# Mix weights of a decoder step: the second half of w_out stays on the chip, the rest passes through one buffer, and TensorE spreads the sample's rows

## What is computed

```python
xn = rms_norm(x, g_mix)
z = xn @ w_in                       # q, k, v of A and B, gates ga, gb
oa, ob, state = mix_fn(qa, ka, va, qb, kb, vb, sink)
ya = oa.reshape(n, s, WIDTH_A) @ w_a          # 512 x 1024
yb = ob.reshape(n, s, WIDTH_B) @ w_b          # 512 x 1024
merged = jax.nn.sigmoid(ga) * ya + jax.nn.sigmoid(gb) * yb
h = x + merged @ w_o                          # 1024 x 1024
hn = rms_norm(h, g_ffn)
y = h + peer(hn.reshape(n * s, D_MODEL), w_pq, sub_keys, u_tab, v_tab).reshape(n, s, D_MODEL)
...
u = jnp.take(u_tab, eb, axis=0)               # peer: per token 128 rows of 1024
act = jax.nn.gelu(jnp.einsum('cd,ced->ce', xb, u, preferred_element_type=jnp.float32), approximate=False)
v = jnp.take(v_tab, eb, axis=0)
out = jnp.einsum('ce,ced->cd', (gb * act).astype(v.dtype), v, preferred_element_type=jnp.float32)
```

## Time and profile before

| | us |
|---|---|
| median of three runs (lowest, highest) | 2066.01 (2065.30, 2066.04) |
| the profiled execution | 2062.75 |
| its span in the trace | 2061.0 |
| TensorE busy | 1453.5 (71%) |
| VectorE busy | 1210.7 (59%) |
| GpSimd busy (issuing the gathers) | 1153.9 (56%) |
| ScalarE busy | 370.2 (18%) |
| traffic of the 16 DMA engines | 710.66 MB, mean 345 GB/s |
| granted clock of TensorE, mean | 0.842 of 2.4 GHz |

### The profile page before, as it was taken

The page is one execution under the profiler, slowest core; times in us unless marked ns, Lnnn a source line. Parts: engine busy times, 40 slices in busy tenths (PEclk is TensorE's granted clock), DMA queues, the critical chain, the costliest instruction groups (busy, mean ns, idle before and its releaser), DMA issues.

```text
span 2061.0 us, 18791 instructions
## 1 busy us (share of the span) xinstructions
PE 1453.5 (71%) x5438; PEld 653.7 (32%) x5438; DVE 1210.7 (59%) x3332; ACT 370.2 (18%) x905; POOL 1153.9 (56%) x1082
## 2 busy tenths in 40 slices
PE   8999898956947495858975566656556767644557
PEld 5443343543423252323332222222222323211111
DVE  1033351497666477656657667677667777776440
ACT  2113342322222121111111111111111111100000
POOL 2020000146656566665777777777677676767764
PEclk9999999967968697789998787888779888777779
DMA  9999987688998889999999999999999999999997
GB/s 335 362 326 370 355 276 245 222 283 316 400 396 326 311 328 379 360 365 370 367 378 383 345 356 356 350 372 364 330 355 363 339 352 348 363 374 382 353 357 276
DMA packets 227303, 710.66 MB, mean 345 GB/s; under 512 B 21288, under 2 KB 46792, under 8 KB 227176
## 3 DMA queue, kind: packets, MB, share of 16 engines
q0 software_dynamic: 166912, 612.40, 79.8%
q1 hardware_dynamic: 60288, 97.05, 13.6%
HBM read 704.84 MB, written 72.65 MB: 377 GB/s over the span
## 4 chain that ended last, share of the span: by engine, by line
PE 30%; issue 26%; DMA 14%; POOL 13%; DVE 10%; another core or an unknown queue 3%; ACT 2%; POOLq 1%; SPq 0%; DVEq 0%; ACTq 0%
PE bank L991 8%; POOL WR L618 7%; POOL XS L618 5%; DMA arena<-in_peer_u_dram,e_all 4%; PE bank L880 4%; DMA XS<-in_peer_u_dram,e_all 4%; DMA WR<-in_peer_v_dram,arena 4%; PE bank L1008 4%; DVE XS L1377 3%; PE bank L1086 3%; PE bank L1107 2%; POOL arena L618 2%; PE bank L1128 2%; PE bank L910 1%
## 5 line engine op out<-in xcount | busy, mean ns | idle before, releaser
L991 PE MATMUL bank<-WR,arena 128*64 128x512 f32 x2048 | 662.1, 753 | 372.6 <-DMA WR<-in_peer_v_dram,arena 245.6
L618 POOL DMA_INDIRECT WR<-in_peer_v_dram,arena x512 | 572.8, 1119 | 249.0 <-issue 161.2
L1377 DVE SCALAR_TENSOR_TENSOR XS<-XS,GT 128x1024 f32<-128x1024 f32 x384 | 465.4, 1225 | 290.8 <-DMA XS<-in_peer_u_dram,e_all 268.3
L618 POOL DMA_INDIRECT XS<-in_peer_u_dram,e_all x384 | 412.2, 1073 | 316.1 <-issue 123.3
L991 PEld LDWEIGHTS bank<-WR,arena 128*64 128x64 f32 x2048 | 184.6, 168 | 790.5 <-issue 752.1
L1377 DVE SCALAR_TENSOR_TENSOR arena<-arena,GT 128x1024 f32<-128x1024 f32 x128 | 157.0, 1226 | 23.4 <-DMA arena<-in_peer_u_dram,e_all 19.5
L618 POOL DMA_INDIRECT arena<-in_peer_u_dram,e_all x128 | 123.2, 963 | 42.2 <-issue 37.1
L1008 PE MATMUL bank<-WR,XS 128*128 128x512 f32 x256 | 118.1, 616 | 12.1 <-ACT GT L746 11.6
L880 PE MATMUL bank<-WR,XS 128*128 128x512 f32 x256 | 112.0, 595 | 0.0
L693 ACT ACTIVATE XS<-bank 128x256 f32<-128x256 f32 (+1 forms) x90 | 36.1, 403 | 361.2 <-remote 190.1
L932 PE MATMUL bank<-arena,PP 128*128 128x64 f32 x272 | 41.8, 282 | 69.2 <-issue 43.7
(11 more groups left out here) (208 smaller groups left out, 1694.7 us busy)
## 6 DMA issues: line engine op xcount, KB each, us to landing
out_dram<-in_cache_a_k_dram POOLq DMA_DIRECT2D x8, 4064.0 KB, 53.0
out_dram<-in_cache_a_v_dram POOLq DMA_DIRECT2D x8, 4064.0 KB, 52.4
WR<-in_w_in_dram SPq DMA_DIRECT2D x8, 2048.0 KB, 24.3
GT<-in_w_peer_q_dram SPq DMA_DIRECT2D x14, 1024.0 KB, 7.2
WR<-in_w_out_dram SPq DMA_DIRECT2D x6, 2048.0 KB
WR<-in_peer_v_dram,arena POOLq DMA_INDIRECT x512
WR<-in_w_branch_a_dram SPq DMA_DIRECT2D x6, 1024.0 KB
WR<-in_w_branch_b_dram SPq DMA_DIRECT2D x6, 1024.0 KB
```

The source lines that it names most:

```text
L618: nc.gpsimd.indirect_dma_start(dst, None, table, bass.IndirectOffsetOnAxis(ap=idx, axis=0))\
L991: last = nc.tensor.matmul(b[c][R * j:R * j + R, :], diag[v % 4][:, s % 4, :], V[V_AT[s]][:, c * CHUNK:(c + 1) * CHUNK], start=False, stop= ...
L1377: V_.scalar_tensor_tensor(u, u, 1.0, hidden[q // TILE_Q], ALU.mult, ALU.mult, accum_out=dots[:, s // TOPK % 4, s % TOPK:s % TOPK + 1]).the ...
```

## The change

1. **w_out's second half** is loaded into w_mix[1] in batch 0 and stays. The two loads of it for batches 1 and 2 are gone.
2. **The branch weights** of batches 1 and 2, both halves, go through w_mix[0]: half 1 is loaded once branches(t, 0) of the batch's last tile is done, then half 0 of w_out once branches(t, 1) is done. In SyncE's queue half 1 of batch 1 moves from behind half 0 to behind query_weights(5), and half 1 of batch 2 from behind half 0 to behind norm_final (L565), ahead of x_again(2).
3. **The mix pieces move** to other slots, and out(t, 1) comes before out(t, 0). post(3), the turn of tile 3's attention, moves from slot 70 to 69. The counts of the semaphore merged follow.
4. **The sample's rows** are spread by TensorE: in slots 143 to 149, sample_rows(b) is for each half one matmul of 512 columns with the identity's column b, broadcast to 128 columns, as the stationary side (8 partitions deep), and one copy by ScalarE of the bank into hbc. The copy's semaphore hb takes the place of the loads' hb_in. hn_scratch, its write and the eight broadcasts are gone.

Slots of the pieces, before and after (br0 is branches(t, 0) and so on):

| tile | before: br0, br1, merged, out0, out1 | after: br0, br1, merged, out1, out0 |
|---|---|---|
| 0 | 17, 18, 19, 19, 20 | 17, 18, 19, 19, 20 (out0 first, as before) |
| 1 | 38, 39, 41, 42, 43 | 38, 40, 42, 43, 44 |
| 2 | 55, 56, 58, 74, 75 | 67, 72, 73, 74, 75 |
| SAMPLE | 70, 71, 73, 76, 77 | 68, 72, 74, 75, 76 |
| 3 | 72, 73, 75, 78, 79 | 70, 73, 74, 75, 77 |

```diff
-    for t, (a, b, c, d, e) in {0: (17, 18, 19, 19, 20), 1: (38, 39, 41, 42, 43), 2: (55, 56, 58, 74, 75),
-                               SAMPLE: (70, 71, 73, 76, 77), 3: (72, 73, 75, 78, 79)}.items():
+    for t, (a, b, c, e, d) in {0: (17, 18, 19, 20, 19), 1: (38, 40, 42, 43, 44), 2: (67, 72, 73, 74, 75),
+                               SAMPLE: (68, 72, 74, 75, 76), 3: (70, 73, 74, 75, 77)}.items():
...
+    for b in range(DEC):
+        put(head_at(SAMPLE, PH - 1) + 1 + min(b, 6), "sample_rows", b)
...
             def branch_weights(batch, c):
+                b = c if batch == 0 else 0
                 if batch == 0:
                     filled(sp, "gate", GATES - 1 - (1 - c) * ALL, 0)
+                elif c == 0:
+                    filled(sp, "out", BATCHES[batch - 1][-1], 0, 0)
                 else:
-                    filled(sp, "out", BATCHES[batch - 1][-1], c, 0)
+                    filled(sp, "branches", BATCHES[batch][-1], 0, 1)
...
             def out_weights(batch, c):
-                filled(sp, "branches", BATCHES[batch][-1], c, 1)
+                filled(sp, "branches", BATCHES[batch][-1], c if batch == 0 else 1, 1)
...
             branch_weights(1, 0)
-            branch_weights(1, 1)
...
             for n in range(3, 6):
                 query_weights(n)
+            branch_weights(1, 1)
             out_weights(1, 0)
-            out_weights(1, 1)
             x_again(1)
             query_weights(6)
             query_weights(7)
             branch_weights(2, 0)
-            branch_weights(2, 1)
...
             query_weights(PH + 2)
-            x_again(2)
...
             sp.dma_start(gfin, g_fin.partition_broadcast(P)).then_inc(S["gfin_in"], 16)
+            branch_weights(2, 1)
+            x_again(2)
             x_again(SAMPLE)
             out_weights(2, 0)
-            out_weights(2, 1)
...
-            for b in range(DEC):
-                sp.dma_start(hbc[b], hn_scratch[b, :].partition_broadcast(P)).then_inc(hb_in[b], 16)
...
+                    elif stage == "sample_rows":
...
+                        for c in range(2):
+                            b = filled(act, "sample_rows", at[0], c)
+                            nc.scalar.activation(hbc[at[0]][:, c * CHUNK:(c + 1) * CHUNK], b[:, :], ACT.Copy).then_inc(S["hb"], 1)
...
+                        for c in range(2):
+                            b, landed = take("sample_rows", r, c)
+                            nc.tensor.matmul(b[:, :], ident[0:DEC, r:r + 1].to_broadcast([DEC, P]),
+                                             hidden[SAMPLE][0:DEC, c * CHUNK:(c + 1) * CHUNK], start=True, stop=True).then_inc(landed, 1)
```

More of the change, by code:

```diff
@@ L144 @@
 USES = {"gate": 1, "gate_sum": 1, "turned": 4, "post": 2, "sample_soft": 2, "sample_turn": 1, "sample_back": 1, "branches": 2, "merged": 2, "out": 1,
-        "hidden": 2, "query": 1, "score": 1, "sample_turn_lists": 2}
+        "hidden": 2, "query": 1, "score": 1, "sample_turn_lists": 2, "sample_rows": 2}
 def tensor_order(pieces, beside):
@@ L196 @@
 BATCH = {t: i for i, ts in enumerate(BATCHES) for t in ts}
-MIX_ORDER = {t: i for i, t in enumerate((0, 1, 2, SAMPLE, 3))}
+MERGED = {0: 2, 1: 4, 2: 8, SAMPLE: 9, 3: 10}
 def ring(slots, buffers):
@@ L360, in hybrid_step_kernel @@
         v_landed = [sem(f"v_landed{j}") for j in range(VR)]
-        hb_in = [sem(f"hb_in{b}") for b in range(DEC)]
         block = ctx.enter_context(nc.Block())
@@ L582, in _ @@
             answer(1)
-            sp.wait_ge(S["hn"], ALL)
-            sp.dma_start(hn_scratch, hidden[SAMPLE][0:DEC, :]).then_inc(S["hn_out"], 16)
             answer(2)
-            sp.wait_ge(S["hn_out"], 16)
-            filled(sp, "query", SAMPLE, PH - 1, 0)
-            for b in range(DEC):
-                sp.dma_start(hbc[b], hn_scratch[b, :].partition_broadcast(P)).then_inc(hb_in[b], 16)
             answer(3)
```

29 lines of the change are left out of this document (18 added, 11 removed).

## The result

| | before | after |
|---|---|---|
| median (lowest, highest), four runs each | 2065.66 (2054.88, 2066.04) | 2093.22 (2085.74, 2099.64) |
| the profiled execution, its span | 2062.75, 2061.0 | 2085.74, 2083.9 |

The ratio of after to before is 1.0145 (95% interval 1.0116 to 1.0175): slower by 1.5%, 20 us above the forecast of 2073, 13 us above 2080, the upper end of the forecast's own range, and 8 us above 2085, the end of the whole range. The direction was right, the size was not: +27.6 us instead of +7.

The account below looks back on a forecast made before the run. Gathers bound the kernel, paced by DMA at 11.96 us a slot, with TensorE the other limit from 931 to 1050 us. Terms 0 − 3 − 2 + 18.5 − 7 = +6.5, about +7 on the 2066.01 median: 2073, range 2056 to 2085.

Parts of the forecast that it names:

- part 2: Batch 2's loads, 561 to 608 us: 2.1 MB fewer, −3; two branches pieces leave slots 55 and 56, −2.
- part 1: Batch 1's loads, near 357 and 500 us: 0; query weights 8 us later, their wait priced in the next term.
- Part 3: Slot 68 on VectorE: SAMPLE's gating waits for gb_in, gathers resume near 928 instead of 917.2: +11 (9.7 to 12).
- Part 4: Slots 70 to 79 on TensorE: bunched wide pieces make slot 80 22.6 us late; +18.5 together with Part 3.
- if it never waits from there: Condition in Part 4: TensorE, 7.5 us late at slot 72 with one piece more, is +15 at slot 80.
- +28: Most for Parts 3 and 4 together, in us, if TensorE falls to the low clock in the gaps.
- The relief: Kept weights and loads, 4.2 MB, fall where gathers stand still: 4 us given back of 10.5, within +18.5.
- Part 5: Sample's rows, 1790 to 1834 us: eight broadcasts, 4.2 MB, gone, −7 (0 to −10.5); added matmuls and copies hidden.
- (b): Rival: low clock, slot 75 stalls VectorE too, part 2 gives nothing: +19, 2085 (2080 to 2091); chance 0.13.
- (a): Rival: late resume made up by TensorE in slots 70 to 79, slot 80 only 3 us late: −9, 2057; chance 0.22.
- (c): Rival: every byte counts over the whole run, 8.4 MB less give 24.3 us: 2042; chance 0.05.
- (d): Rival: nearly nothing, gb_in is in time or late sample rows at slots 157 and 158 cancel the gain: 2066; chance 0.10.

Follow-up runs that it names:

- e6: Changed kernel with query_weights(6) issued ahead of batch 1's w_out half 0 and x_again(1): 2093.61 us, 1.0085 of before.
- e10: Changed kernel with gate_b[SAMPLE] loaded first, out pieces one a slot, and query_weights(6) ahead of w_out: 2073.03 us, 0.9980 of before.
- e16: e10's three edits to the changed kernel, plus batch 2's branches and merged pieces spread, one wide piece a slot from 72: 2064.75 us, 1.0010 of before.
- e14: Changed kernel with the 32 KB load gate_b[SAMPLE] issued ahead of kept_weights(6) and w_q7: 2085.07 us, 1.0104 of before.

## Why the prediction was wrong, by its own steps

**Parts 1 and 2: predicted −5, measured −0.7 at slot 69** (after was 3.7 late at slot 29, where the runs differ by as much anyway; counted from there it is −4.4 in this pair of traces and about 0 over all of them). The step that failed is the estimate that the query weights come 8 us later, with a wait that costs no more than part 2 gives back. They landed 15.3 us later, at 558.6 instead of 543.25. Of that, 12.4 us is the issue (529.70 instead of 517.29), a whole slot, which part 1 had named as the most before it took 8. Another 2.9 us is the load: from issue to use it took 28.9 us, and 26.0 in before. TensorE also came to the query 2.2 us earlier, since out(1, 0) no longer stands ahead of it. Together with the 0.23 us of before that is the wait of 17.8. The gain was real, some 6 to 7 us once the wait is gone (e6, e10, e16).

**Part 3: predicted +10.7, measured +9.8 at slot 70**, +10.5 in slot 69's length. The cause was right, and e14 confirms it. That the times agree to a microsecond (919.3 for 920, 927.0 for 928) is in part luck. VectorE and SyncE were there 3 us earlier than in before (908.3 for 911.3, 910.57 for 913.85), and the small load took 8.7 us from its issue where 6.2 were worked out; the wait was 10.94 us and not 9.

**Part 4 was the large mistake: predicted 22.6 late at slot 80 with part 3, measured 33.8.** Slot 75 held as forecast: 24.8 us from 1012.61, for 25. The start of slot 72 did not, though its number did: it was worked out as 956 from late gathers that let slot 71's accumulation end there, and came at 956.85. But that accumulation had ended at 949.1, 7 us ahead of the forecast, and TensorE then stood for branch half 1, which was issued at 938.4 and waited for 7.77 us. Part 4 had named that load and given its wait no price; two errors met in one number by luck. What was left out from there is small waits. The accumulations of slots 72 to 77 ended at 978.5, 998.7, 1012.7, 1037.3, 1047.9 and 1063.7; the forecast had 974, 990, 1004, 1029, 1040 and 1055. So 4.5 us were lost in slot 72 and 4.2 more in slot 73, then nothing to slot 77, and 2.2 in 78 and 79. They are the second branches piece's wait for its banks (2.31), the wait for ScalarE's copy of the turned merged(2) (3.28), and 1.6 and 1.7 us for the pieces that ran at a granted clock of 0.82 and 0.80. The step that failed is "if it never waits from there": the chain of slots 72 and 73 has no term for TensorE's waits for banks. The earlier trace rows had shown one of the same kind, 3.66 us and then a piece of 9.94. The +28 that was given as the most for parts 3 and 4 was too low, since it was built on the same chain.

**The relief: 4 predicted, 3.5 measured** (33.8 at slot 80, 30.3 at slot 100). **Part 5: −7 predicted, −5.8 measured** in slots 142 to 144 (30.8 to 25.0); the added work was hidden as said, at 0.60 us a copy. Later slots and the tail changed little: 26.7 at slot 157, 22.9 at the end.

**Medians.** The profiled executions differ by 23.0 us, the medians by 27.6; the profile of after is the fastest of its four runs. So of the 20 us above the forecast, 16 are the terms (11 of part 4, 4 of parts 1 and 2, 1 of part 5), and about 4 the scatter of runs, which spread over 14 us in after and more in other groups. The range had no room for it.

**Rivals.** (b) was nearest, and half of it is what happened: slot 75 held up VectorE too (it waited 6.63 and 6.04 us for the outs there) and in after the wait for the query weights ate what part 2 gives. Its other half, a low clock through the gaps, came only for two pieces and some 3 us, and before has one such piece too; the granted clock is 0.97 in 965 to 1080 us. I had added its price, 19, to the same undersized chain and given it 0.13. (a) fell, since TensorE could not make the late resume good; (c) fell with it: 8.4 MB fewer and 27.6 us more. (d) fell for the gate, and for the rows.

## What to carry to other kernels

Where queues are in order and rings let the transfers lead by one step only, the wide pieces' places count more than their sum: the same ten pieces cost 11 to 13 us more when three stand in one slot. A small load that gates an in-order engine goes ahead of large ones in its queue. A load that is released by a piece moves by the whole slot when the piece moves by one, and every load behind it in the queue moves with it. Two pieces that share banks wait for whoever empties these, so that engine's place in the slot needs a term in the sum. A change that saves bytes and moves work is two changes: here the part that moved none of the pieces (the rows) was the gain.
